# Column vectors laid out by the host, filler turns on TensorE, and a last down projection that finishes quarter by quarter

## The chip, the cores and the metric

One core of one Trainium2 chip runs the program; the other cores are idle. The metric is device time in microseconds of that core, as the median of several runs. The kernel before takes 1831.78 us (median of three runs, 1830.54 to 1832.52). A profile is one further execution of the same program; times inside it count from the start of its span.

## The reference

The function takes x, 256 positions of 2048 fp32 values, through three blocks. The first two (MLA attention, sliding-window attention with sinks) compute `x = x + (y * silu(gate)) @ w_out` on a normalised input. The third runs one more normalised mixer (block attention and a state space part), and then a gated feed-forward block whose output is normalised before it is added to x. What the change touches is the first normalisation,

```
h = rmsnorm(x, layer_norm[0])            # x * rsqrt(mean(x^2) + eps) * g
proj = h @ mla_w_in
```

the small vectors that are used as one scalar per feature (gains of norms, the filters and offsets of two depthwise convolutions), and the very end,

```
down = hidden @ w_ffn_down               # (256, 5632) @ (5632, 2048)
x = x + rms_norm(down, ln_ffn_post)      # gain, and 1/sqrt(mean(down^2) + eps) per row
return x
```

## The kernel before, in words

Every weight matrix streams through TensorE in tiles of 128x1024 fp32. SyncE issues the load of a tile into one of four `raw` slots. ScalarE rounds it to `w_high` (line 1163), VectorE forms `w_low = raw - w_high` (line 1662) and adds one to the semaphore `low_made`. TensorE then multiplies three times (high by high, high by low, low by high) and adds one to `tiles_used`, which frees the slots. `split(tile)` on ScalarE and VectorE always runs three tiles ahead (LEAD = 3). Activations are split into high and low parts in the same way. Each engine has its own program, written out by hand, and the engines meet at semaphores only, so an instruction that waits holds up everything behind it on its engine.

**The start.** SyncE loads the two halves of x (`x_in`), then weight tiles. ScalarE's queue loads the identity matrix (`ident_in`, line 1255) and half of the small vectors, one DMA each, as rows of `vector_rows` (line 1257); GpSimd's queue loads the other half (line 2448). TensorE waits for all of them and turns six groups of rows into columns in PSUM (line 621). VectorE copies those into `column_vectors` (lines 1773 to 1779, with a factor 0.5 on two parts) and adds to `cols_done`; only behind that, on the same engine, stands `normalise0` (line 1675), which scales most of x by its roots. ScalarE scales the rest (line 1188). `transpose_rows` on TensorE turns the scaled x in 32 turns of 128x128 (line 545), four to a PSUM bank. Of each bank ScalarE makes `hT_high` (line 1225) and VectorE `hT_low` (line 1679). The first weight tile is multiplied (lines 515 to 517) behind the 32 turns and once `hl_done` is 2, that is, once two banks have low parts.

**The end.** The down projection sums over 44 chunks of the hidden layer into all eight PSUM banks. Bank 4t + g holds rows t (0 or 1, 128 rows each) and columns 512g to 512g + 511. `down_step` takes 8 tiles: tiles 0 to 3 are the left half of the columns for four chunks, tiles 4 to 7 the right half. In the last step (`last_down_step`) tiles 4 to 7 are multiplied first for t = 0, which completes banks 2 and 3 (`first_rows`), then for t = 1, which completes banks 6 and 7. Behind that stands the output of the block. For each bank ScalarE takes the sum of squares (line 1644, semaphore `sq`) and VectorE the product with the gain into `nx` (line 2437, semaphore `scaled`). The two engines go through the banks in different orders (`ACT_TAIL`, `DVE_TAIL`), and each waits for the other before it takes a bank that the other one had. For rows t, VectorE then adds four sums (line 2418), GpSimd makes the root `rstd` (lines 2568, 2569), VectorE computes `x = nx * rstd + x` in four pieces (line 2423, semaphore `fin`), and SyncE stores each piece (line 491).

Of the kernel before, what the change touches and what calls it, by code (L numbers as in the profile page):

```python
# [24 lines left out]
F32 = mybir.dt.float32  # L25
# [55 lines left out]
LINE = 32  # L81
FIRST_IN = ((T_C, 0), (T_KR, 16), (T_MLAO + LEAD, 0), (T_KV, 16), (T_SWAO + LEAD, 0), (T_XBC, 16),
# [119 lines left out]
def program(nc, a, out, toeplitz):  # L202
# [9 lines left out]
    with ctx:  # L212
# [50 lines left out]
        rows = sb("vector_rows", [P, 6, P], F32, s0)  # L263
# [91 lines left out]
        def column(slot, at):  # L355
# [4 lines left out]
        row_loads = [(0, V_LN0, a["layer_norm"]), (0, V_QN, a["q_norm"]), (0, V_KVN, a["kv_norm"]),  # L360
                     (0, V_MIX, a["ln_mix_pre"]), (0, V_FFN, a["ln_ffn_pre"]), (0, V_SSMN, a["ssm_norm"]),
                     (0, V_XB, a["conv_b"]), (1, 0, a["conv_w"]), (2, 0, a["ffn_b"])]
        row_loads += [(3 + k, 0, a["ffn_w"][88 * k:88 * (k + 1), :]) for k in range(3)]
        N_ROWS = len(row_loads)
# [4 lines left out]
        consts_in, ident_in, vec_in, rows_in = sem("consts_in"), sem("ident_in"), sem("vec_in"), sem("rows_in")  # L369
        rows_in_act, masks_made = sem("rows_in_act"), sem("masks_made")  # L370
# [3 lines left out]
        cols_psum, cols_done, trig_angle, trig_done = sem("cols_psum"), sem("cols_done"), sem("trig_angle"), sem("trig_done")  # L374
# [22 lines left out]
        ff = names("ffn", "ups", "acc", "taps", "gelu", "hidden", "split", "sq", "rs", "scaled", "first_rows", "fin")  # L397
# [3 lines left out]
        DVE_TAIL = (4, 5, 0, 1, 3, 2, 7, 6)  # L401
# [14 lines left out]
        def _(sp):  # L416
# [80 lines left out]
        def _(pe):  # L497
# [614 lines left out]
            def down_rows(i, j, t):  # L1112
# [5 lines left out]
                for k in range(2):  # L1118
# [8 lines left out]
            def last_down_step(i):  # L1127
# [22 lines left out]
        def _(act):  # L1150
# [105 lines left out]
            for slot, row, src in row_loads[:len(row_loads) // 2]:  # L1256
                act.dma_start(rows[row:row + src.shape[0], slot, :], src).then_inc(rows_in_act, 16)
# [4 lines left out]
            normalise1(1)  # L1262
            act.wait_ge(cols_done, 1)
# [383 lines left out]

        @block.vector
        def _(dve):
# [119 lines left out]
            dve.wait_ge(cols_psum, 1)  # L1769
            for slot, n in enumerate((V_SLOT0, 48, FC * 2, FC * 2, FC * 2, FC * 2)):  # L1770
# [831 lines left out]
```

## Time and profile before

| | us |
|---|---|
| median of three runs | 1831.78 |
| the profiled execution, its own time | 1830.33 |
| its span | 1828.5 |
| TensorE busy | 1790.7 |
| VectorE busy | 1139.2 |
| ScalarE busy | 896.3 |
| first weight multiplied | 21.44 |
| last matmul starts | 1819.87 |

"Busy" is the union of an engine's instructions. TensorE appears twice, as PE (the matmuls) and PEld (the loads of its stationary operand, which overlap the matmuls). The duration of a matmul in a row contains its way through the array, so two that follow each other overlap: the distance between starts is what each costs. A row of the timeline gives the start, the duration, the engine, the line, what is written and read, how many instructions are merged, and in brackets how long the engine was idle before and what released it.

### The profile page before, as it was taken

Reading aid. Unit: us, or ns where it says so; the run is one execution under the profiler, and the core shown is the slowest. Engines: PE = TensorE matmul, PEld = TensorE weight load, DVE = VectorE, ACT = ScalarE, POOL = GpSimd, SP = SyncE. Lnnn points to the kernel's source line nnn. Section 1 sums busy time; section 2 is a strip of 40 time slices with the busy share of each in tenths; the row PEclk is TensorE's granted clock in tenths of the full one; section 3 lists DMA queues with packets and bytes.
Section 4 is the critical chain, followed back from the end, with each engine's and each line's share of the span. In section 5 each row is a group of like instructions: output and inputs, shape, how many; then the busy total and the mean of one; then the engine's idle time right before and its main releaser. Section 6 shows DMA issues by size and latency. Waiting matters only on the chain. (4 is left out here: it accounts for less than half of the span.)

```text
span 1828.5 us, 35122 instructions
## 1 busy us (share of the span) xinstructions
PE 1790.7 (98%) x13052; PEld 1671.4 (91%) x13052; DVE 1139.2 (62%) x1790; ACT 896.3 (49%) x1350; POOL 154.3 (8%) x189
## 2 busy tenths in 40 slices
PE   6999999999999999999999999999999999999998
PEld 5999998899999788999999779999999999988886
DVE  6665555656777766766565556666666666644445
ACT  6555454555544555454444445444554444433333
POOL 1001110000100101000000000100000000033321
PEclk9999999999999999999999999999999999999999
DMA  7555555565454455665564655666656666666554
GB/s 234 168 166 152 162 156 173 183 181 179 145 158 155 148 187 168 186 192 168 171 179 144 208 160 178 193 197 192 194 184 189 190 198 193 199 197 193 192 193 139
DMA packets 235612, 326.46 MB, mean 179 GB/s; under 512 B 12432, under 2 KB 170420, under 8 KB 234896
## 3 DMA queue, kind: packets, MB, share of 16 engines
q1 hardware_dynamic: 233440, 318.61, 56.5%
q0 software_dynamic: 1808, 6.69, 1.2%
q8 instruction: 52, 0.85, 0.2%
q14 instruction: 24, 0.20, 0.0%
q10 hardware_dynamic: 288, 0.11, 0.0%
HBM read 323.24 MB, written 2.13 MB: 178 GB/s over the span
## 5 line engine op out<-in xcount | busy, mean ns | idle before, releaser
L1662 DVE TENSOR_TENSOR w_low<-raw,w_high 128x1024 fp32r<-128x1024 f32 x603 | 736.1, 1230 | 573.0 <-ACT w_high L1163 571.4
L1163 ACT CAST w_high<-raw 128x1024 fp32r<-128x1024 f32 x603 | 626.9, 1049 | 645.3 <-PE bank L509 330.4
L507 PE MATMUL bank<-hT_high,w_high 128*128 128x256 f32 x2608 | 728.6, 279 | 6.1 <-DVE hT_low L1679 2.8
L509 PE MATMUL bank<-hT_high,w_low 128*128 128x256 f32 x2608 | 722.7, 277 | 0.0
L508 PE MATMUL bank<-hT_low,w_high 128*128 128x256 f32 x2608 | 722.7, 277 | 0.0
L507 PEld LDWEIGHTS bank<-hT_high,w_high 128*128 128x128 f32 x2608 | 490.8, 188 | 13.2 <-issue 5.8
L509 PEld LDWEIGHTS bank<-hT_high,w_low 128*128 128x128 f32 x2608 | 490.6, 188 | 0.0
L508 PEld LDWEIGHTS bank<-hT_low,w_high 128*128 128x128 f32 x2608 | 490.4, 188 | 0.1
L515 PE MATMUL bank<-w_high,yT_high 128*128 128x512 f32 x384 | 152.2, 396 | 4.8 <-POOL yT_low L2464 2.8
L517 PE MATMUL bank<-w_high,yT_low 128*128 128x512 f32 x384 | 149.8, 390 | 0.0
L516 PE MATMUL bank<-w_low,yT_high 128*128 128x512 f32 x384 | 149.8, 390 | 0.0
L1124 PE MATMUL bank<-w_high,hidden_low 128*128 128x512 f32 x264 | 102.7, 389 | 0.0
L1122 PE MATMUL bank<-w_high,hidden_high 128*128 128x512 f32 x264 | 102.7, 389 | 0.0
L1123 PE MATMUL bank<-w_low,hidden_high 128*128 128x512 f32 x264 | 102.7, 389 | 0.0
L515 PE MATMUL bank<-w_high,hT_high 128*128 128x256 f32 (+1 forms) x320 | 96.8, 303 | 0.0
L516 PE MATMUL bank<-w_low,hT_high 128*128 128x256 f32 (+1 forms) x320 | 96.1, 300 | 0.0
L517 PE MATMUL bank<-w_high,hT_low 128*128 128x256 f32 (+1 forms) x320 | 96.0, 300 | 0.0
L515 PEld LDWEIGHTS bank<-w_high,yT_high 128*128 128x128 f32 x384 | 72.1, 188 | 22.0 <-issue 4.0
L517 PEld LDWEIGHTS bank<-w_high,yT_low 128*128 128x128 f32 x384 | 72.1, 188 | 15.5
L516 PEld LDWEIGHTS bank<-w_low,yT_high 128*128 128x128 f32 x384 | 72.1, 188 | 14.5
L2553 POOL COPY hidden_staged<-hidden_T 128x512 f32 (+1 forms) x22 | 14.5, 658 | 610.7 <-DVE hidden_T L2371 474.7
L2463 POOL CAST yT_high<-y_rows 128x256 f32 (+3 forms) x28 | 17.4, 622 | 552.2 <-DVE y_rows L1833 442.1
(322 smaller groups left out, 2166.7 us busy)
## 6 DMA issues: line engine op xcount, KB each, us to landing
raw<-in_w_up SPq DMA_DIRECT2D x176, 512.0 KB, 4.5
raw<-in_w_in SPq DMA_DIRECT2D x88, 512.0 KB, 3.7
raw<-in_w_down SPq DMA_DIRECT2D x88, 512.0 KB, 4.4
raw<-in_w_swa SPq DMA_DIRECT2D x72, 512.0 KB, 4.1
raw<-in_w_c SPq DMA_DIRECT2D x50, 512.0 KB, 3.8
raw<-in_w_mlao SPq DMA_DIRECT2D x32, 512.0 KB, 3.7
raw<-in_w_swao SPq DMA_DIRECT2D x32, 512.0 KB, 4.4
raw<-in_w_out SPq DMA_DIRECT2D x32, 512.0 KB, 4.0
```

The costliest lines, as they stand in the source:

```text
L507: nc.tensor.matmul(to, h, act_h[:, chunk, :], start=first, stop=False, skip_group_check=True)
L508: nc.tensor.matmul(to, h, act_l[:, chunk, :], start=False, stop=False, skip_group_check=True)
L509: return nc.tensor.matmul(to, l, act_h[:, chunk, :], start=False, stop=last, skip_group_check=True)
L515: nc.tensor.matmul(to, ah, h, start=first, stop=False, skip_group_check=True)
L516: nc.tensor.matmul(to, ah, l, start=False, stop=False, skip_group_check=True)
L517: return nc.tensor.matmul(to, al, h, start=False, stop=last, skip_group_check=True)
L1122: nc.tensor.matmul(to, ah, wh[:, w], start=first, stop=False, skip_group_check=True)
L1123: nc.tensor.matmul(to, ah, wl[:, w], start=False, stop=False, skip_group_check=True)
L1124: last = nc.tensor.matmul(to, al, wh[:, w], start=False, stop=True, skip_group_check=True)
L1163: nc.scalar.copy(whi(tile, i, n), raw[s][:, :]).then_inc(high_made, 1)
L1662: v.tensor_tensor(wlo(tile, i, n), raw[s][:, :], whi(tile, i, n).bitcast(F32), ALU.subtract).then_inc(low_made, 1)
L2463: chain.done(g_.tensor_copy(h, y32[:, 0:n, :]))
```

## The change

Four things change.

The host lays all small vectors out as one array of shape 128 x 6 x 96, as `column_vectors` has it. ScalarE's queue loads the first of the six parts, GpSimd's queue the other five in one DMA; `vector_rows`, its six turns and its copies are gone. VectorE only halves two parts in place.

TensorE runs 44 turns of the identity matrix into bank 7 as soon as `ident_in` has come, ahead of the 32 real turns. Nobody reads them.

In the last down step tiles 4 to 7 are multiplied for one bank at a time: bank 2, bank 3, bank 6, bank 7. `first_rows` now counts the first three.

In the output, VectorE takes the banks in the order in which they are completed, and waits for ScalarE's square of a bank before its own product. The sums and outputs of rows 0 and 1 stand at new places in VectorE's program. The first of the four output pieces of rows 1 is no longer VectorE's: ScalarE multiplies `nx` by the root in place, GpSimd adds x, and SyncE stores that piece third of four.

```diff
+WARM = 44
-        DVE_TAIL = (4, 5, 0, 1, 3, 2, 7, 6)
+        DVE_TAIL = (4, 5, 0, 1, 2, 3, 6, 7)
@@ SyncE
-            for b in range(8):
-                sp.wait_ge(ff["fin"], b + 1)
-                t, g = b // 4, b % 4
+            for n, (t, g) in enumerate(((0, 0), (0, 1), (0, 2), (0, 3), (1, 1), (1, 2), (1, 0), (1, 3))):
+                if (t, g) == (1, 0):
+                    sp.wait_ge(ff["fin_pool"], 1)
+                else:
+                    sp.wait_ge(ff["fin"], n + 1 if n < 6 else 7)
                 sp.dma_start(out[t * P:(t + 1) * P, g * 512:(g + 1) * 512],
@@ TensorE, start
             pe.wait_ge(ident_in, 16)
-            pe.wait_ge(rows_in_act, 16 * (N_ROWS // 2))
-            pe.wait_ge(rows_in, 16 * (N_ROWS - N_ROWS // 2))
-            for slot, n in enumerate((V_SLOT0, 48, 2 * FC, 2 * FC, 2 * FC, 2 * FC)):
-                last = nc.tensor.transpose(banks[slot // 3][:, (slot % 3) * P:(slot % 3) * P + n], rows[0:n, slot, :], ident[0:n, 0:n])
-            last.then_inc(cols_psum, 1)
-            pe.wait_ge(cols_done, 1)
+            for _ in range(WARM):
+                flip(banks[7][:, 0:P], ident)
             transpose_rows()
@@ TensorE, last_down_step (down_rows takes the halves k to do as ks)
-                for j in range(4, 8):
-                    ready(T_DOWN + j, i, 8)
-                    last = down_rows(i, j, 0)
-                last.then_inc(ff["first_rows"], 1)
-                for j in range(4, 8):
-                    down_rows(i, j, 1).then_inc(tiles_used, 1)
+                for t in range(TT):
+                    for k in range(2):
+                        for j in range(4, 8):
+                            if t + k == 0:
+                                ready(T_DOWN + j, i, 8)
+                            last = down_rows(i, j, t, (k,))
+                            if t + k == 2:
+                                last.then_inc(tiles_used, 1)
+                        if t + k < 2:
+                            last.then_inc(ff["first_rows"], 1)
@@ ScalarE, start and output
-            for slot, row, src in row_loads[:len(row_loads) // 2]:
-                act.dma_start(rows[row:row + src.shape[0], slot, :], src).then_inc(rows_in_act, 16)
+            act.dma_start(colv[:, 0, :], a["columns"][:, 0, :]).then_inc(cols_first, 16)
...
-                if n == 4:
-                    act.wait_ge(ff["first_rows"], 1)
-                if n == 6:
+                if n in (4, 5, 6):
+                    act.wait_ge(ff["first_rows"], n - 3)
+                if n == 7:
                     act.wait_ge(tiles_used, T_END)
-                if n in (2, 5, 7):
+                if n == 2:
                     act.wait_ge(ff["scaled"], n)
...
+            act.wait_ge(rstd_done, RSTD_TAIL + 1)
+            act.wait_ge(ff["scaled"], 8)
+            nc.scalar.activation(nx[:, 1, 0:512], nx[:, 1, 0:512], ACT.Copy, scale=rstd[:, 1:2]).then_inc(ff["times_r"], 1)
@@ VectorE, start
-            dve.wait_ge(cols_psum, 1)
-            for slot, n in enumerate((V_SLOT0, 48, FC * 2, FC * 2, FC * 2, FC * 2)):
...
-            last.then_inc(cols_done, 1)
+            dve.wait_ge(cols_first, 16)
+            v.tensor_scalar(colv[:, 0, V_XB:V_SLOT0], colv[:, 0, V_XB:V_SLOT0], 0.5, None, ALU.mult)
+            dve.wait_ge(cols_rest, 16)
+            v.tensor_scalar(colv[:, 1, 0:48], colv[:, 1, 0:48], 0.5, None, ALU.mult).then_inc(cols_done, 1)
             normalise0(1)
@@ VectorE, output (output_rows without its sum, which is row_sums)
+                if n in (2, 4, 5, 6):
+                    dve.wait_ge(ff["sq"], 2 if n == 2 else n + 1)
+                if n == 5:
+                    row_sums(0, 6)
                 if n == 6:
-                    output_rows(0, 6)
-                    dve.wait_ge(tiles_used, T_END)
-                if n in (2, 5, 7):
-                    dve.wait_ge(ff["sq"], n)
-                t, cols = b // 4, slice(b % 4 * 512, (b % 4 + 1) * 512)
-                v.tensor_tensor(nx[:, t, cols], banks[b], gbc[:, cols], ALU.mult).then_inc(ff["scaled"], 1)
-            output_rows(1, 8)
+                    output_rows(0, 6, 0)
+                if n == 7:
+                    row_sums(1, 8)
+                scaled_by_gain(b)
+            output_rows(1, 8, 1)
@@ GpSimd, start and output
-            for slot, row, src in row_loads[len(row_loads) // 2:]:
-                pool.dma_start(rows[row:row + src.shape[0], slot, :], src).then_inc(rows_in, 16)
+            pool.dma_start(colv[:, 1:6, :], a["columns"][:, 1:6, :]).then_inc(cols_rest, 16)
...
+            pool.wait_ge(ff["times_r"], 1)
+            g_.tensor_tensor(x[:, 1, 0:512], nx[:, 1, 0:512], x[:, 1, 0:512], ALU.add).then_inc(ff["fin_pool"], 1)
```

The instruction lists below name an instruction by its line, what it writes and reads, its size, and in brackets the semaphores that it waits for.

TensorE's program at the start, before (the first rows below the start of the block):

```order
L621 MATMUL bank0<-constants,vector_rows 128x92 [waits rows_in,rows_in_act,ident_in]
L621 MATMUL bank0<-constants,vector_rows 128x48
L621 MATMUL bank0<-constants,vector_rows 128x88
L621 MATMUL bank1<-constants,vector_rows 128x88 x3
L545 MATMUL bank0<-constants,nx 128x128 [waits nx_done,cols_done]
```

The same place after the change:

```order
L541 MATMUL bank7<-constants 128x128 [waits ident_in]
L541 MATMUL bank7<-constants 128x128 x43
L541 MATMUL bank0<-constants,nx 128x128 [waits nx_done]
L541 MATMUL bank0<-constants,nx 128x128 x3
L541 MATMUL bank1<-constants,nx 128x128 [waits nx_done]
```

Six turns of vector rows have given way to 44 of the identity, and the first real turn waits for scaled x alone.

VectorE's program at the end, before, from the first product with the gain (`scores` are banks 4 and 5):

```order
L2437 TENSOR_TENSOR nx<-scores,gain_rows 128x512 [waits tiles_used,gain_in]
...
L2437 TENSOR_TENSOR nx<-bank,gain_rows 128x512 [waits ffn_first_rows]
L2437 TENSOR_TENSOR nx<-bank,gain_rows 128x512 [waits ffn_sq]
L2418 TENSOR_REDUCE sum_squares<-small 128x1 [waits ffn_sq]
L2423 SCALAR_TENSOR_TENSOR x<-nx,rstd,x 128x512 [waits rstd_done,ffn_scaled]
L2423 SCALAR_TENSOR_TENSOR x<-nx,rstd,x 128x512 x3
L2437 TENSOR_TENSOR nx<-bank,gain_rows 128x512 [waits tiles_used]
L2437 TENSOR_TENSOR nx<-bank,gain_rows 128x512 [waits ffn_sq]
L2418 TENSOR_REDUCE sum_squares<-small 128x1 [waits ffn_sq]
L2423 SCALAR_TENSOR_TENSOR x<-nx,rstd,x 128x512 [waits rstd_done,ffn_scaled]
L2423 SCALAR_TENSOR_TENSOR x<-nx,rstd,x 128x512 x3
```

The same place after the change, from bank 2 on:

```order
L2423 TENSOR_TENSOR nx<-bank,gain_rows 128x512 [waits ffn_sq]
L2409 TENSOR_REDUCE sum_squares<-small 128x1 [waits ffn_sq]
L2423 TENSOR_TENSOR nx<-bank,gain_rows 128x512
L2417 SCALAR_TENSOR_TENSOR x<-nx,rstd,x 128x512 [waits rstd_done,ffn_scaled,ffn_sq]
L2417 SCALAR_TENSOR_TENSOR x<-nx,rstd,x 128x512 x3
L2423 TENSOR_TENSOR nx<-bank,gain_rows 128x512
L2409 TENSOR_REDUCE sum_squares<-small 128x1 [waits ffn_sq]
L2423 TENSOR_TENSOR nx<-bank,gain_rows 128x512
L2417 SCALAR_TENSOR_TENSOR x<-nx,rstd,x 128x512 [waits rstd_done,ffn_scaled]
L2417 SCALAR_TENSOR_TENSOR x<-nx,rstd,x 128x512 x2
```

The reduction of each half has moved ahead of the product of that half's last bank. The four outputs of rows 0 now wait for a third semaphore, `ffn_sq`: its count is 7, ScalarE's square of bank 6. The product of bank 6 stands behind them.

TensorE's program in the last down step, tiles 4 to 7 (in slots 3, 0, 1, 2), before, without the rows of line 1123:

```order
L1122 MATMUL bank2<-w_high3,hidden_high 128x512 [waits low_made]
...
L1122 MATMUL bank3<-w_high3,hidden_high 128x512
...
L1122 MATMUL bank2<-w_high0,hidden_high 128x512 [waits low_made]
...
L1122 MATMUL bank3<-w_high0,hidden_high 128x512
...
L1122 MATMUL bank2<-w_high1,hidden_high 128x512 [waits low_made]
...
L1122 MATMUL bank3<-w_high1,hidden_high 128x512
...
L1122 MATMUL bank2<-w_high2,hidden_high 128x512 [waits low_made]
```

The same place after the change:

```order
L1114 MATMUL bank2<-w_high3,hidden_high 128x512 [waits low_made]
...
L1114 MATMUL bank2<-w_high0,hidden_high 128x512 [waits low_made]
...
L1114 MATMUL bank2<-w_high1,hidden_high 128x512 [waits low_made]
...
L1114 MATMUL bank2<-w_high2,hidden_high 128x512 [waits low_made]
...
L1114 MATMUL bank3<-w_high3,hidden_high 128x512
```

Between the first matmul of tile 4 and that of tile 7 there stood 18 matmuls; now there stand 9.

## Rows read from the trace of the kernel before

**Rows 1.** The page: busy time, share of the span, instructions, of each engine.

```profile
PE 1790.7 (98%) x13052; PEld 1671.4 (91%) x13052; DVE 1139.2 (62%) x1790; ACT 896.3 (49%) x1350; POOL 154.3 (8%) x189
```

**Rows 2.** Waits in 12 to 26 us: in total, times, longest.

```profile
PE bank L621 <- DMA vector_rows<-in_ssm_norm: 12.1, 1, 12.1
PE bank L545 <- DVE nx L1675: 2.0, 1, 2.0
```

**Rows 3.** Timeline of the start: start, duration, instruction, idle before.

```profile
9.35 1.91 ACT L1260 ACTIVATE nx<-x 128x2048 f32<-128x2048 f32 x1 [0.58 <-DMA x<-in_x]
12.48 1.95 ACT L1188 ACTIVATE nx<-x,rstd 128x512 f32<-128x512 f32 x3 [1.13 <-POOL rstd L2456]
13.57 0.24 DVE L1775 COPY column_vectors<-bank 128x80 f32<-128x80 f32 x1 [13.57 <-PE bank L621]
14.55 2.22 DVE L1675 TENSOR_SCALAR nx<-x,rstd 128x512 f32<-128x512 f32 x5
15.54 3.28 PEld L545 LDWEIGHTS bank<-constants,nx 128*128 128x128 f32 x16 [2.27 <-DVE column_vectors L1779]
16.69 1.70 ACT L1225 ACTIVATE hT_high<-bank,column_vectors 128x256 fp32r<-128x256 f32 x4 [0.98 <-PE bank L545]
17.92 1.65 DVE L1679 SCALAR_TENSOR_TENSOR hT_low<-bank,column_vectors,hT_high 128x256 fp32r<-128x256 f32 x4
18.80 1.72 PEld L545 LDWEIGHTS scores<-constants,nx 128*128 128x128 f32 x8
20.50 0.94 PEld L545 LDWEIGHTS bank<-constants,nx 128*128 128x128 f32 x8
21.42 0.19 PEld L515 LDWEIGHTS bank<-w_high,hT_high 128*128 128x128 f32 x1
```

**Rows 4.** The identity's DMA on ScalarE's queue: its issue, and time to landing.

```profile
L1255 ACTq DMA_DIRECT2D constants<-in_constants x1: 387/387/387, 1.9 to 1.9; - x1
DMA to landing us min/median/max: 8.0/8.0/8.0
```

**Rows 5.** Timeline of TensorE at 1085 us: turns of the identity.

```profile
1085.30 4.09 PE L545 MATMUL scores<-constants 128*128 128x128 f32 x36
```

**Rows 6.** Stretches: busy of PE, PEld, DVE, ACT, POOL, then granted clock, DMA share, GB/s.

```profile
12.00:15.50 3.50, 1.43 (x6) 0.94 (x6) 1.93 (x10) 2.78 (x4) 0.45 (x1) 1.00 1.03 414
18.80:20.62 1.82, 1.82 (x10) 1.82 (x10) 1.82 (x4) 1.82 (x5) 0.00 (x0) 1.00 0.82 203
```

**Rows 7.** Timeline of the last down step and the output.

```profile
1809.22 0.39 PE L1122 MATMUL bank<-w_high,hidden_high 128*128 128x512 f32 x1
1809.47 1.05 ACT L1163 CAST w_high<-raw 128x1024 fp32r<-128x1024 f32 x1 [1.67 <-PE scores L1124]
1810.55 1.23 DVE L1662 TENSOR_TENSOR w_low<-raw,w_high 128x1024 fp32r<-128x1024 f32 x1 [1.49 <-ACT w_high L1163]
1817.50 2.74 DVE L2423 SCALAR_TENSOR_TENSOR x<-nx,rstd,x 128x512 f32<-128x512 f32 x4 [1.04 <-POOL rstd L2569]
1819.87 0.39 PE L1124 MATMUL bank<-w_high,hidden_low 128*128 128x512 f32 x1
1820.30 1.41 DVE L2437 TENSOR_TENSOR nx<-bank,gain_rows 128x512 f32<-128x512 f32 x2
1821.02 0.60 ACT L1644 ACTIVATE hT_high<-bank 128x512 fp32r<-128x512 f32 x1
1821.74 0.16 DVE L2418 TENSOR_REDUCE sum_squares<-small 128x1 f32<-128x4 f32 x1
1822.92 2.74 DVE L2423 SCALAR_TENSOR_TENSOR x<-nx,rstd,x 128x512 f32<-128x512 f32 x4 [1.02 <-POOL rstd L2569]
1825.02 0.99 SPq L491 DMA_DIRECT2D out<-x  x2
```

**Rows 8.** GpSimd's two-input operations on 512 columns: count, busy, mean ns, idle.

```profile
L2555 POOL TENSOR_TENSOR hidden_low<-hidden_staged,hidden_high 128x512 fp32r<-128x512 f32 x22 | 44.7, 2034 | 1.8
L2464 POOL TENSOR_TENSOR yT_low<-y_rows,yT_high 128x512 fp32r<-128x512 f32 x4 | 5.1, 1284 | 0.3
```

More of the change, by code:

```diff
@@ L357, in column @@
             return colv[:, slot, at:at + 1] if isinstance(at, int) else colv[:, slot, bass.ds(at, 1)]
[L360 to L364, printed above, removed]
         raw_loaded = [sem(f"raw_loaded{s}") for s in range(SLOTS)]
         high_made, low_made, tiles_used = sem("high_made"), sem("low_made"), sem("tiles_used")
-        consts_in, ident_in, vec_in, rows_in = sem("consts_in"), sem("ident_in"), sem("vec_in"), sem("rows_in")
-        rows_in_act, masks_made = sem("rows_in_act"), sem("masks_made")
+        consts_in, ident_in, vec_in, cols_first = sem("consts_in"), sem("ident_in"), sem("vec_in"), sem("cols_first")
+        cols_rest, masks_made = sem("cols_rest"), sem("masks_made")
         x_in = [sem("x_in0"), sem("x_in1")]
@@ L396, in program @@
                    "gated", "ss", "rstd", "yn", "y_tr", "y_high", "y_low")
-        ff = names("ffn", "ups", "acc", "taps", "gelu", "hidden", "split", "sq", "rs", "scaled", "first_rows", "fin")
+        ff = names("ffn", "ups", "acc", "taps", "gelu", "hidden", "split", "sq", "rs", "scaled", "first_rows", "fin", "times_r", "fin_pool")
+        RSTD_TAIL = 7
         ACT_TAIL = (0, 1, 4, 5, 2, 3, 6, 7)
-        DVE_TAIL = (4, 5, 0, 1, 3, 2, 7, 6)
+        DVE_TAIL = (4, 5, 0, 1, 2, 3, 6, 7)
         def start(eng, *groups):
@@ L1117, in down_rows @@
                 al = hidl[:, chunk // 2, chunk % 2, t * P:(t + 1) * P]
-                for k in range(2):
+                for k in ks:
                     to = banks[4 * t + 2 * half + k]
@@ L1262, in _ @@
             normalise1(1)
+            act.wait_ge(cols_first, 16)
             act.wait_ge(cols_done, 1)
@@ L1766, in angles @@
                 v.scalar_tensor_tensor(turns[:, :], ang[:, :], -1.0, ang[:, :], ALU.mult, ALU.max).then_inc(trig_angle, 1)
-            dve.wait_ge(cols_psum, 1)
-            for slot, n in enumerate((V_SLOT0, 48, FC * 2, FC * 2, FC * 2, FC * 2)):
-                src = banks[slot // 3][:, (slot % 3) * P:(slot % 3) * P + n]
-                if slot == 1:
-                    last = v.tensor_scalar(colv[:, 1, 0:n], src, 0.5, None, ALU.mult)
-                elif slot == 0:
-                    v.tensor_copy(colv[:, 0, 0:V_XB], src[:, 0:V_XB])
-                    last = v.tensor_scalar(colv[:, 0, V_XB:n], src[:, V_XB:n], 0.5, None, ALU.mult)
-                else:
-                    last = v.tensor_copy(colv[:, slot, 0:n], src)
-            last.then_inc(cols_done, 1)
+            dve.wait_ge(cols_first, 16)
+            v.tensor_scalar(colv[:, 0, V_XB:V_SLOT0], colv[:, 0, V_XB:V_SLOT0], 0.5, None, ALU.mult)
+            dve.wait_ge(cols_rest, 16)
+            v.tensor_scalar(colv[:, 1, 0:48], colv[:, 1, 0:48], 0.5, None, ALU.mult).then_inc(cols_done, 1)
             normalise0(1)
@@ L2414, in _, with row_sums, output_rows @@
             dve.wait_ge(gain_in, 48)
-            def output_rows(t, squared):
+            def row_sums(t, squared):
                 dve.wait_ge(ff["sq"], squared)
                 v.reduce_sum(ss[:, t:t + 1], small[:, 4 * t:4 * t + 4], axis=AX.X).then_inc(ff["rs"], 1)
-                dve.wait_ge(ff["scaled"], squared)
-                dve.wait_ge(rstd_done, 7 + t)
-                for g in range(4):
+            def output_rows(t, scaled, first):
+                dve.wait_ge(ff["scaled"], scaled)
+                dve.wait_ge(rstd_done, RSTD_TAIL + t)
+                for g in range(first, 4):
                     cols = slice(g * 512, (g + 1) * 512)
@@ L2424, in output_rows, with scaled_by_gain @@
                                            ALU.mult, ALU.add).then_inc(ff["fin"], 1)
+            def scaled_by_gain(b):
+                t, cols = b // 4, slice(b % 4 * 512, (b % 4 + 1) * 512)
+                v.tensor_tensor(nx[:, t, cols], banks[b], gbc[:, cols], ALU.mult).then_inc(ff["scaled"], 1)
             for n, b in enumerate(DVE_TAIL):
@@ L2569, in _, with vectors_as_columns @@
                 g_.tensor_tensor(rstd[:, one], rstd[:, one], nhalf[:, one], ALU.pow).then_inc(rstd_done, 1)
+            pool.wait_ge(ff["times_r"], 1)
+            g_.tensor_tensor(x[:, 1, 0:512], nx[:, 1, 0:512], x[:, 1, 0:512], ALU.add).then_inc(ff["fin_pool"], 1)
+def vectors_as_columns(f):
+    slots = [["layer_norm", "mla_q_norm", "mla_kv_norm", "ln_mix_pre_2", "ln_ffn_pre_2", "ssm_norm_w_2", "ssm_conv_b_2"],
+             ["ssm_conv_w_2"], ["ffn_conv_b_2"]]
+    laid = [np.concatenate([f(name).reshape(-1, P) for name in slot]) for slot in slots]
+    laid += list(f("ffn_conv_w_2").reshape(3, 2 * FC, P))
+    out = np.zeros((P, 6, 96), np.float32)
+    for slot, part in enumerate(laid):
+        out[:, slot, :part.shape[0]] = part.T
+    return out
 def kernel(**inputs):
@@ L2581 @@
         "constants": shape_constants(),
[L2582 to L2586 removed]
+        "columns": vectors_as_columns(f),
         "final_norm": f("final_norm").reshape(1, D), "ln_mix_post": f("ln_mix_post_2").reshape(1, D),
```

12 lines of the change are left out of this document (2 added, 10 removed).

## The prediction

> **What bounds the kernel now.** I read the page first. TensorE is busy for 1790.7 of 1828.5 us, 98% of the span, while VectorE is at 62% and ScalarE at 49% [rows 1]. No edit touches the number of matmuls that matter or their pace in between, so only two places can move the time: the 21.4 us ahead of the first weight, and what lies behind the last matmul. I then read the waits and the timeline of the first 26 us. TensorE idles for 12.1 us until the last rows of vectors land and another 2.0 us for scaled x [rows 2]. Scaled x is late because VectorE copies columns from 13.57 and begins to scale at 14.55 only, while the roots were there for ScalarE at 12.48 [rows 3]. From 15.54 on TensorE turns without a pause and the first weight follows at 21.42 [rows 3]: the turns themselves set that moment, not `hl_done` (VectorE's low parts of the first two banks run 17.92 to 19.57).
>
> The pace of the turns matters. Eight loads take from 18.80 to 20.50, 0.2125 us each; the eight behind them take 0.94 us, and 36 turns at 1085 us take 4.09 us, which without the last one's 0.27 us way through the array is 0.11 us each [rows 3, 5]. The granted clock reads 1.00 in the slow stretch too [rows 6], so the column doesn't show it; a factor of two in the pace of equal work is TensorE at 1.2 and then at 2.4 GHz, with the rise at 20.50, after 4.96 us of unbroken turns, or 8.4 us after the first rows were turned at about 12.1. By the Trainium skill ("TensorE: Matmul & The Clock Gate", "What's actually happening") the clock is either of these two and nothing between; rows 3 and 5 agree, the clock column doesn't.
>
> At the end the last matmul starts at 1819.87 and is through at 1820.26. Products and squares of banks 6 and 7 take until 1821.74, sum and root until 1822.92, four outputs until 1825.66, and the last store is issued at 1825.69 (two issues in 0.99 us from 1825.02, 0.33 each) [rows 7]. The span ends 2.81 us later, at 1828.5. From the last matmul to the end it is 8.24 us.
>
> **The start, part by part.** The vector DMAs: nothing but the columns themselves hangs on them now. VectorE's two halvings can wait for them only if they land after 12.48; the identity, first on the same queue as before, was issued at 1.88 and landed 8.0 us later, at 9.9 [rows 4], and the last rows of before, issued much later, had landed at 12.1. I cost this at nothing. If the one larger GpSimd transfer did land late, the fillers below would hide up to some 3.5 us of it. The copies on VectorE go, so scaling starts at 12.5 in place of 14.55: two microseconds that would all come back if TensorE stood ready.
>
> It doesn't. The 44 fillers start with the identity at 9.9. With a slow stretch of 4.96 us, 23.3 of them run at 0.2125 us; the other 20.7 take 2.28 us at 0.11. They end at 17.1. Scaled x has been complete since about 14.9 (12.5 + 2.22 + what ScalarE adds). The 32 real turns take 3.52 us at 0.11, so the first weight comes at 20.64, 0.78 us earlier than 21.42. Behind it: the first bank is turned at about 17.8, and by the distances of rows 3 (ScalarE 16.69, VectorE's fourth low part at 19.57, at most 2.9 us) `hl_done` is 2 by 20.4 to 20.7, just in time. **I take 0.8 us gained.**
>
> Bounds. If the clock counts from the first work of all, 8.4 us slow: 39.5 fillers slow, 4.5 fast, end at 18.8, first weight at 22.3, a loss of 0.9. All 76 turns slow: 16.15 us, first weight at 26.0, a loss of 4.6. All fast: 8.36 us, first weight at 18.3, a gain of 3.2. I take the unbroken 4.96 us, since the six turns of before were followed by 2 us of idling and the fillers are not. A second unknown is when the identity lands: GpSimd's queue now puts 246 KB of columns and then the positions beside x early, where it spread them before. At 400 GB/s [rows 6] 280 KB more ahead of it are 0.7 us, straight from the gain.
>
> **The end, part by part.** *The last tile is asked for too early.* Tiles 4 to 7 were 18 matmuls apart from first to last, now 9. At 0.227 us (48 matmuls of 0.227 from 1809.22 give the end) TensorE wants tile 7 at 1809.22 + 9 x 0.227 = 1811.26. ScalarE can round it only from 1809.47, when its slot is free, and VectorE has its low part at 1810.55 + 1.23 = 1811.78 [rows 7]. Before, it was wanted at 1813.3 and this was hidden. So TensorE stops for 0.5 us and more: I take 0.55, and all four quarters end that much later, the last at 1820.81. Ends: 0.3 (if the release comes ahead of the modelled end of the operation) and 0.75 (if the 0.19 us of a weight load come on top).
>
> *VectorE's queue.* With quarters 2.72 us apart, bank 6 is complete at 1818.09 and squared 0.75 us later, at 1818.84 (before, 0.72 from 1820.30 to 1821.02). The outputs of rows 0 now wait for that square. Before they ran at 1817.50. They take 2.74, until 1821.58, and the product of bank 6 stands behind them (0.7, until 1822.28), and the sum of rows 1 behind that. ScalarE has squared bank 7 by 1821.56, so the sum waits for VectorE, not for ScalarE. From a sum to the first output it is 1.18 us (1821.74 to 1822.92): outputs of rows 1 begin at 1823.46, against 1822.92. The product of bank 7 hides in those 1.18 us. The freed swap of banks (0.7) is given back here. Three outputs instead of four end at 1825.53, against 1825.66.
>
> *The piece on ScalarE and GpSimd.* ScalarE needs the same root: 1823.46, plus 0.7 (a third of 1.95 and its tail [rows 3]), plus 0.1 for the hand-over, is 1824.26. GpSimd then adds 512 columns of two inputs. It took 2.03 us beside a VectorE that read two inputs for half of the time, and 1.28 us in four others [rows 8]. Here VectorE's outputs read two inputs until 1825.53, so I take 2.15, a bit above the mean, and keep 1.28 as the low end; GpSimd is done at 1826.41 (1825.54). The Trainium skill ("GPSIMD Engine Reference", "Engine selection") says outright that elementwise work of two inputs belongs on VectorE, GpSimd being about twice as slow, and ("Specifications") that VectorE's two-input instructions contend with it. By that alone, twice VectorE's 0.67 us would be some 1.35 us, and contention more; row 8 has both.
>
> *The stores.* SyncE stores that piece third of four and waits for it, so the last store, ready at 1825.53, is issued behind it: 1826.44 + 0.33 = 1826.77, against 1825.69, that is 1.08 later. Two stores of 256 KB now leave 0.33 us apart where it was 0.67, so the last queues by another 0.35 or so. **The end costs 1.4 us** (1.08 + 0.35), 0.55 of it the stop of TensorE. Ends: 0.2 (GpSimd at 1.28, a stop of 0.3, little queueing) and 1.8.
>
> **The sum.** -0.8 + 1.4 = +0.6 us. On the profiled execution's 1830.33 that is 1830.9; the median of before lies 1.45 above that execution, so on its scale I expect 1831.78 + 0.6 = 1832.4. Anything within 3.66 us (0.2%) is no change, about what a measurement of this kernel can tell.
>
> **The rivals.** *A: the warm start pays in full.* The clock rises early in the fillers, or the identity lands well before 9.9. Then the first weight comes up to 3.2 us earlier. With the cost at the end: 1831.78 - 3.2 + 1.4 = 1830.0; with the cheapest end, 1828.8; only with the identity also 1 us early is it past 0.2%. For it: the pace doubled within one turn in before, so a rise can be anywhere. Against it: 4.96 us of unbroken work were not enough until 20.50.
>
> *B: the end pays.* GpSimd is at 1.28 us and TensorE hardly stops: +0.2 - 0.8, 1831.2. For it: four rows at 1.28. Against: 22 rows at 2.03, and VectorE active beside it.
>
> *C: the fillers run slow to the last one, and the real turns as well.* One mechanism, in front of the first weight: TensorE stays at 1.2 GHz through turns of 128 columns. Price 4.6 us, plus 1.4: 1837.8, slower. It is past 0.2% once the first weight comes later than about 23.7, that is, once the slow stretch lasts 11 us. For it: before ran slow until 8.4 us after its first work. Against it: the unbroken part of that was 4.96 us.
>
> *D: the slow stretch lasts 8.4 us,* by the same evidence: +0.9 + 1.4, 1834.1.
>
> **How the numbers follow.** The forecast, with its own range of 1831.0 to 1833.5: 64%. A: 12%, B: 10%, D: 7%, C: 4%; 3% for what I don't see. The two ends outside 0.2% are C, and A where all its luck comes together. The range has to take in A at 1830.0, D at 1834.1, and the 2 us by which the three runs of before differ among themselves: 1829.6 to 1834.8. Faster by over 0.2%: 6%; within: 88%; slower: 6%.
>
> **What would show it.** The first weight between 20 and 21.2 us, ahead of it turns at 0.11, and fillers that start at 9.9 and double their pace midway. A gap of about 0.5 us in TensorE ahead of the matmuls of tile 7. Outputs of rows 0 that begin behind the square of bank 6 and end after the last matmul; VectorE's last sum more than 1 us behind the last matmul; GpSimd's addition ending after VectorE's last output; the last store issued 6 us after the last matmul (before 5.4). I am wrong if the fillers are over by 14 us, if TensorE doesn't stop at tile 7, or if rows 0 are out before bank 6 is squared.

## The result, and the profile after

The kernel before takes 1830.69 us (median of 20 runs, 1829.6 to 1834.11), the changed one 1833.43 us (20 runs, 1832.15 to 1836.54). The ratio is 1.0014, 95% interval 1.0008 to 1.002: 2.7 us or 0.14% slower, inside the 0.2% that the prediction called no change, and on the side of its +0.6 us. In the runs of the last experiments two timings, 5644.21 us (e10) and 2581.43 us (the kernel before beside it), lie far out; they count in the medians and not in the ratios. The profiled executions differ by 2.85 us: 1833.18 against 1830.33 in their own time, spans 1831.1 against 1828.5.

I cut both traces at two moments, the first weight and the end of the last matmul (start plus 0.39 us):

| us | before | after | difference | forecast |
|---|---|---|---|---|
| start of the span to the first weight | 21.42 | 23.01 | +1.59 | -0.78 |
| first weight to the end of the last matmul | 1798.84 | 1799.71 | +0.87, of it 0.71 the stop at tile 7 | +0.55 |
| end of the last matmul to the end of the span | 8.24 | 8.38 | +0.14 | +0.85 |
| outside the span | 1.83 | 2.08 | +0.25 | 0 |
| sum | 1830.33 | 1833.18 | +2.85 | +0.62 |

The start. Timeline of the changed kernel, one engine after the other (start, duration, instruction, idle before), to be read beside [rows 3]:

```profile
5.63 1.91 ACT L1255 ACTIVATE nx<-x 128x2048 f32<-128x2048 f32 x1 [1.36 <-DMA x<-in_x]
10.50 1.91 ACT L1255 ACTIVATE nx<-x 128x2048 f32<-128x2048 f32 x1 [2.87 <-DMA x<-in_x]
13.63 1.95 ACT L1184 ACTIVATE nx<-x,rstd 128x512 f32<-128x512 f32 x3 [1.13 <-POOL rstd L2454]
12.99 0.17 DVE L1769 TENSOR_SCALAR column_vectors<-column_vectors 128x12 f32<-128x12 f32 x1 [12.99 <-DMA column_vectors<-in_columns]
13.63 2.07 DVE L1674 TENSOR_SCALAR nx<-x,rstd 128x512 f32<-128x512 f32 x5 [0.37 <-POOL rstd L2454]
11.99 7.55 PEld L541 LDWEIGHTS bank<-constants 128*128 128x128 f32 x44 [11.99 <-DMA constants<-in_constants]
19.52 1.78 PEld L541 LDWEIGHTS bank<-constants,nx 128*128 128x128 f32 x16
23.01 0.19 PEld L511 LDWEIGHTS bank<-w_high,hT_high 128*128 128x128 f32 x1
```

The copies are gone, yet scaling begins at 13.63 and not at 12.5: the second half of x is squared from 10.50 on, where it was 9.35 [rows 3]. The identity lands at 11.99, so the fillers, which need 7.55 us, end at 19.52; scaled x has been complete since 15.7. Between them the fillers hold the real turns up by 3.8 us. The pace is 0.2125 us a turn and then 0.11 [rows 3, 5]: 44 turns in 7.55 us put 26.5 of them at the first pace, 5.6 us.

What landed when, from the DMA issues of the first 14 us (KB each, median us from issue to landing), first the kernel before and then the changed one:

```profile
x<-in_x SPq DMA_DIRECT2D x2, 1024.0 KB, 6.6
positions_i<-in_positions POOLq DMA_DIRECT2D x1, 128.0 KB, 6.6
```

```profile
x<-in_x SPq DMA_DIRECT2D x2, 1024.0 KB, 7.1
column_vectors<-in_columns POOLq DMA_DIRECT2D x1, 240.0 KB, 7.2
positions_i<-in_positions POOLq DMA_DIRECT2D x1, 128.0 KB, 8.3
constants<-in_constants ACTq DMA_DIRECT2D x1, 64.0 KB, 10.1
```

The identity, 8.0 us underway before [rows 4], now needs 10.1. In 5 to 9.2 us GpSimd's queue (q0) takes 45% of the DMA engines where it took 18%, and less is moved in all (335 against 362 GB/s). DMA queues in that stretch (packets, MB, share of 16 engines), before and after:

```profile
q1 hardware_dynamic: 248, 1.23, 75.5%
q0 software_dynamic: 179, 0.21, 18.3%
```

```profile
q1 hardware_dynamic: 151, 1.00, 57.7%
q0 software_dynamic: 92, 0.36, 45.0%
```

The end. Timeline of the changed kernel from the last tile on, to be read beside [rows 7]:

```profile
1811.22 1.05 ACT L1159 CAST w_high<-raw 128x1024 fp32r<-128x1024 f32 x1 [1.67 <-PE scores L1116]
1812.30 1.23 DVE L1661 TENSOR_TENSOR w_low<-raw,w_high 128x1024 fp32r<-128x1024 f32 x1 [1.50 <-ACT w_high L1159]
1812.78 0.39 PE L1116 MATMUL bank<-w_high,hidden_low 128*128 128x512 f32 x1
1813.58 0.50 PE L1114 MATMUL bank<-w_high,hidden_high 128*128 128x512 f32 x1 [0.41 <-DVE w_low L1661]
1820.03 0.60 ACT L1640 ACTIVATE hT_high<-bank 128x512 fp32r<-128x512 f32 x1 [2.03 <-PE bank L1116]
1820.76 2.74 DVE L2417 SCALAR_TENSOR_TENSOR x<-nx,rstd,x 128x512 f32<-128x512 f32 x4 [1.90 <-ACT hT_high L1640]
1822.33 0.39 PE L1116 MATMUL bank<-w_high,hidden_low 128*128 128x512 f32 x1
1823.41 0.68 DVE L2423 TENSOR_TENSOR nx<-bank,gain_rows 128x512 f32<-128x512 f32 x1
1824.01 0.14 DVE L2409 TENSOR_REDUCE sum_squares<-small 128x1 f32<-128x4 f32 x1
1825.11 0.72 ACT L1644 ACTIVATE nx<-nx,rstd 128x512 f32<-128x512 f32 x1 [1.67 <-POOL rstd L2567]
1825.18 3.08 DVE L2417 SCALAR_TENSOR_TENSOR x<-nx,rstd,x 128x512 f32<-128x512 f32 x3 [0.42 <-POOL rstd L2567]
1825.91 1.80 POOL L2569 TENSOR_TENSOR x<-nx,x 128x512 f32<-128x512 f32 x1 [0.83 <-ACT nx L1644]
```

Tile 7 is wanted at 1812.78 + 0.23 = 1813.01; its low part is made until 1813.53, and the matmul starts at 1813.58. (The wait shows as 0.41 us because the row counts from the modelled end of the matmul before.) From the first matmul of tile 4 at 1810.97 to the end of the last it is 11.75 us; in before it is 1819.87 + 0.39 - 1809.22 = 11.04 for the same 48 matmuls [rows 7], so the stop costs 0.71 us. Outputs of rows 0 run from 1820.76, behind the square of bank 6, and hold up the product of bank 6 and, behind it, the sum. The sum runs at 1824.01, 1.29 us behind the end of the last matmul at 1822.72. The piece on ScalarE and GpSimd is done at 1827.71, VectorE's third output only at 1828.26.

### The profile page after: what moved, and what is told of

Same layout as the page of the kernel before. It is cut to its first block and busy times, and to the rows that moved or that the text cites. A ratio compares the mean times of both kernels' runs of the same rounds, so it can differ in the third digit from the quotient of the medians.

```text
span 1831.1 us, 35184 instructions
## 1 busy us (share of the span) xinstructions
PE 1794.7 (98%) x13090; PEld 1675.5 (92%) x13090; DVE 1139.0 (62%) x1784; ACT 896.4 (49%) x1351; POOL 153.9 (8%) x185
```

## The experiments

Each kernel is the changed one with the edit shown (e4 apart); "..." marks what is left out. Where a kernel was timed, its ratio is to the kernel before. "Middle" is the stretch from the first weight to the end of the last matmul, "output" the one from there to the end of the span.

**The start.** *e1: no fillers.*

```diff
-WARM = 44
+WARM = 0
```

> The changed kernel without its 44 filler turns. Theory 1 (the fillers hold back the real turns, for which scaled x is there from about 14.4 us): the real turns start at 14.4, run slow (0.2125 us) for the 5.5 us that the fillers took to speed up, 26 of the 32, then 0.11: first weight at 20.6 us in place of 23.0, span 2.4 us shorter, about 1828.7. Theory 2 (the fillers pay for themselves, what is late is the identity alone): the first weight comes no earlier than 23.0, or comes earlier and its matmuls run at half pace, so that the span is unchanged at 1831. Between them, all 32 turns slow: 21.4.

Measured: 1831.15 us (10 runs) against 1830.82 of before (25 runs), ratio 1.0003 (0.9993 to 1.0013). Weight loads of its trace:

```profile
14.46 3.27 PEld L541 LDWEIGHTS bank<-constants,nx 128*128 128x128 f32 x16 [14.46 <-issue]
17.71 1.53 PEld L541 LDWEIGHTS scores<-constants,nx 128*128 128x128 f32 x8
19.21 0.90 PEld L541 LDWEIGHTS bank<-constants,nx 128*128 128x128 f32 x8
20.09 0.19 PEld L511 LDWEIGHTS bank<-w_high,hT_high 128*128 128x128 f32 x1
```

The real turns begin as soon as scaled x is there, pay the slow stretch themselves (about 22 slow turns, 4.5 us), and still the first weight comes at 20.09. The fillers don't save the slow stretch; they move it ahead, behind a load that lands late, and add their own 44 turns. Against the 23.01 of the changed kernel's trace that is 2.9 us; against e7 (below), which has the same fillers and its first weight at 21.04, it is 1.0. The timings alone don't tell e1 from the changed kernel: each was set against the kernel before in another series, with ratios of 1.0003 (up to 1.0013) and 1.0014 (from 1.0008).

*e2: GpSimd issues the positions and the sinks only when x is in.*

```diff
+            pool.wait_ge(x_in[1], 16)
             pool.dma_start(posi[:, :], a["positions"]
```

> The changed kernel, but GpSimd issues its loads of the positions (128 KB) and of the sinks only once x has landed. Theory 1 (GpSimd's early transfers take turns with x and with the identity): 144 KB less ahead of them, x complete 0.4 us earlier than 10.5 and the identity 0.4 to 1.0 us earlier than 12.0, first weight 0.4 to 1.0 earlier. Theory 2 (the identity is late because of the transfer behind it on ScalarE's queue, or by chance): x at 10.5 and the identity at 12.0 as before.

Start of its timeline:

```profile
9.19 1.91 ACT L1255 ACTIVATE nx<-x 128x2048 f32<-128x2048 f32 x1 [1.30 <-DMA x<-in_x]
9.41 7.18 PEld L541 LDWEIGHTS bank<-constants 128*128 128x128 f32 x44 [9.41 <-DMA constants<-in_constants]
20.05 0.19 PEld L511 LDWEIGHTS bank<-w_high,hT_high 128*128 128x128 f32 x1
```

The identity lands 2.6 us earlier than in the changed kernel's trace and x 1.3 us earlier, by taking 144 KB out of the way. Other traces agree: the identity needs 9.1 to 10.1 us to land in the five with the positions early (the changed kernel, e1, e5, e6, e7) and 7.4 to 7.6 in the four with them late (e2, e8, e9, e10). Their bytes would be about 0.36 us at 400 GB/s [rows 6]. The direction was right, and the size several times what bytes say. The span was 1831.3 all the same: this trace's middle has two spells of half pace that before's hasn't (last section).

*e3: GpSimd issues all its loads when x is in.*

```diff
+            pool.wait_ge(x_in[1], 16)
             pool.dma_start(colv[:, 1:6, :], a["columns"]
```

> The changed kernel, but GpSimd issues all its loads (246 KB of columns, positions, sinks) only once x has landed. Theory 1: nothing of GpSimd's runs beside x, so x is complete by 9.3 us or a bit earlier and the identity lands at 9.9 or earlier (before: 9.9); fillers from there, first weight at 9.9 + 5.5 + 2.0 + 3.5 = 20.9, span 2.1 us shorter than 1831.1, about 1829.0. Risk: the columns land only at 12 to 13 us and hold VectorE's scaling back; the fillers hide up to 3 us of that. Theory 2 (ScalarE's queue or chance): identity at 12.0, no change.

Measured: 1832.28 us (10 runs), ratio 1.0006 (0.9996 to 1.0015). The identity lands at 8.78, and now the columns are late:

```profile
15.40 0.19 DVE L1771 TENSOR_SCALAR column_vectors<-column_vectors 128x48 f32<-128x48 f32 x1 [5.53 <-DMA column_vectors<-in_columns]
16.44 1.73 PEld L541 LDWEIGHTS bank<-constants,nx 128*128 128x128 f32 x16 [0.36 <-DVE nx L1674]
```

VectorE can scale only behind its halving of the columns, so the first weight comes at 20.33. It is the positions that have to move, not the columns.

**The end.** *e4: the kernel before with the new end only* (order of tiles 4 to 7, VectorE's order, the piece and the stores; the start untouched).

```diff
-        DVE_TAIL = (4, 5, 0, 1, 3, 2, 7, 6)
+        DVE_TAIL = (4, 5, 0, 1, 2, 3, 6, 7)
...
+                            last = down_rows(i, j, t, (k,))
...
-            output_rows(1, 8)
+            output_rows(1, 8, 1)
```

> The kernel before with only the new end (quarters, new order on VectorE, one piece on ScalarE and GpSimd). Theory 1 (of the 2.6 us that the span grew, 1.6 are the start, 0.7 a stop of TensorE ahead of tile 7, 0.14 the output): first weight at 21.4, span 1828.5 + 0.85 = 1829.4, last matmul through to end of span 8.4 us. Theory 2 (the end is as good as before and the growth is all the start or the stretch between): span 1828.5.

Measured: 1832.57 us (10 runs), ratio 1.0005 (0.9995 to 1.0015). The trace has the first weight at 21.66 and the same stop at tile 7:

```profile
1812.55 0.39 PE L1127 MATMUL bank<-w_high,hidden_low 128*128 128x512 f32 x1
1813.35 0.50 PE L1125 MATMUL bank<-w_high,hidden_high 128*128 128x512 f32 x1 [0.41 <-DVE w_low L1672]
```

Its output takes 8.62 us. The span is 1831.1; without one such spell in its middle (1.6 us, last section) it would be about 1829.5, near the 1829.4 expected. So the new end alone isn't told apart from before, and neither is the changed kernel without its fillers (e1). The new start with the old end was not run.

*e5: the outputs of rows 0 ahead of the wait for the square of bank 6.*

```diff
+                if n == 6:
+                    output_rows(0, 6, 0)
                 if n in (2, 4, 5, 6):
                     dve.wait_ge(ff["sq"], 2 if n == 2 else n + 1)
                 if n == 5:
                     row_sums(0, 6)
-                if n == 6:
-                    output_rows(0, 6, 0)
```

> The changed kernel, with the four outputs of rows 0 ahead of the wait for ScalarE's square of bank 6 in VectorE's program. Theory 1 (these outputs, started 1.96 us before the last matmul is through, hold back the sum of rows 1): they start 1.2 us after the sum of rows 0, are over before the last matmul, and the sum of rows 1 comes 0.78 us behind the end of the last matmul (now 1.29), so that the span ends 7.9 us behind it (now 8.38). Theory 2 (the output is bound by something later, GpSimd or the stores): the distance from the last matmul to the end stays 8.4. Only distances from the last matmul on count here.

In its trace the last matmul is through at 1825.18, and the sum of rows 1 runs at

```profile
1825.94 0.16 DVE L2409 TENSOR_REDUCE sum_squares<-small 128x1 f32<-128x4 f32 x1 [0.83 <-ACT hT_high L1640]
```

0.76 us behind it, against 1.29 in the changed kernel, and it waits for ScalarE now. Output 7.82 us (8.38 before the edit): the queue on VectorE was real and cost about half a microsecond.

*e6: rows 0 by tile, as before, and only rows 1 by quarters.*

```diff
-                for t in range(TT):
-                    for k in range(2):
-                        for j in range(4, 8):
...
+                for j in range(4, 8):
+                    ready(T_DOWN + j, i, 8)
+                    last = down_rows(i, j, 0)
+                last.then_inc(ff["first_rows"], 2)
+                for k in range(2):
+                    for j in range(4, 8):
+                        last = down_rows(i, j, 1, (k,))
...
```

> The changed kernel, but tiles 4 to 7 of the last down step are multiplied for rows 0 as before (both banks for a tile, then the next tile), and quarter by quarter for rows 1 only. Theory 1 (asking for tile 7 after 9 matmuls in place of 18 costs 0.7 us): no wait on w_low in the last step, and 11.04 us from the first matmul of tile 4 until the last one is through, as before, in place of 11.75; the output behind it unchanged at 8.4 us. Theory 2: the gap only moves, 11.5 or more.

In its trace TensorE waits for no low part any more; first matmul of tile 4 and last matmul:

```profile
1811.36 0.39 PE L1114 MATMUL bank<-w_high,hidden_high 128*128 128x512 f32 x1
1822.01 0.39 PE L1116 MATMUL bank<-w_high,hidden_low 128*128 128x512 f32 x1
```

That is 11.04 us to the end, as expected: the 0.71 us stop comes from the quarters of rows 0 alone. The output behind it is unchanged at 8.40.

*e7: no piece on ScalarE and GpSimd; VectorE does all four outputs, stored in order.*

```diff
-            output_rows(1, 8, 1)
+            output_rows(1, 8, 0)
...
-            nc.scalar.activation(nx[:, 1, 0:512], nx[:, 1, 0:512], ACT.Copy, scale=rstd[:, 1:2]).then_inc(ff["times_r"], 1)
-            g_.tensor_tensor(x[:, 1, 0:512], nx[:, 1, 0:512], x[:, 1, 0:512], ALU.add).then_inc(ff["fin_pool"], 1)
```

> The changed kernel, but VectorE makes all four outputs of rows 1, with nothing on ScalarE and GpSimd and the stores in order. Theory 1 (GpSimd's addition makes VectorE's last output take 1.75 us in place of 0.75, so the fourth piece elsewhere gains nothing): four outputs of 0.67 us, over 2.74 us after their start in place of 3.08, and 8.0 us from the last matmul to the end in place of 8.38. Theory 2 (a piece taken off VectorE is a piece gained): 0.67 us more on VectorE than its present 3.08, so 9.0 us.

Its trace:

```profile
1825.31 2.74 DVE L2411 SCALAR_TENSOR_TENSOR x<-nx,rstd,x 128x512 f32<-128x512 f32 x4 [0.42 <-POOL rstd L2561]
```

VectorE makes four outputs in 2.74 us where three beside GpSimd took 3.08 (in the changed kernel and in e1 to e6 alike). Output 7.95 us against 8.38: the piece, with its place in the stores, costs 0.4 us.

**All of it together.** *e8 has the edits of e1, e2, e5, e6 and e7; e9 is the same kernel, timed; e10 has 16 fillers (`WARM = 16`) in place of none.*

> Columns from the host kept; no fillers; positions and sinks loaded only once x is in; rows 0 of the last step by tile; rows 0 out before the wait for bank 6; four outputs on VectorE. Theory 1: x at 9.2, real turns from 13.3, first weight 5.6 us later at 18.9; 1798.8 us to the end of the last matmul as in the kernel before, if the clock stays up between; 7.55 us of output (sum at 0.78, first output 1.18 later, 2.74 for four, 2.85 to the end). Span 1825.3, plus 1.2 to 1.7 for each stretch in the middle in which TensorE's clock falls. Theory 2 (parts overlap, what one gives another takes): 1827.5 or more even with the clock up.

> The kernel of e8 again, timed, since a single run can't tell 3 us from the stretches of low clock in the middle. Theory 1 (start 2.7 us and output 0.8 us shorter than in the kernel before, nothing given back): median 3.0 to 3.5 us below the kernel before and 5.5 to 6.5 below the changed kernel. Theory 2 (an earlier first weight is lost again in the middle, as e2 and e3 could be read, where the first weight came 1.4 and 1.1 us earlier than in before and the span was longer): median no more than 1 us below the kernel before.

> The kernel of e9 with 16 fillers ahead of the real turns. Theory 1 (fillers are good as far as they end before scaled x is there, at 13.3 us): they start with the identity at 9.4, run slow until 12.8, the clock rises 3.9 to 5.5 us after their start, at 13.3 to 14.9, so that most real turns are fast; then the low parts of the first two banks set the first weight, about 18.0, 0.7 us earlier than without fillers. Theory 2 (the pause of half a microsecond between fillers and real turns undoes them): turns slow for another 4 us, first weight at 18.7 or later.

e8: first weight 18.70, output 7.42, span 1825.7 (1825.3 expected). e9: 1828.35 us (11 runs) against 1831.55 of before (21 runs), ratio 0.9983 (0.9974 to 0.9992). e10: 1827.48 us (11 runs), ratio 0.998 (0.997 to 0.9989). So both beat the kernel before, by 3.2 and 4.1 us, and are not told apart from each other. By the segments of its trace e9 gains 3.3 us ahead of the first weight and 0.8 in the output, and loses 0.2 outside the span. How much of the start is owed to the columns from the host, and how much to moving the positions, wasn't separated. e10's weight loads:

```profile
9.33 3.27 PEld L538 LDWEIGHTS bank<-constants 128*128 128x128 f32 x16 [9.33 <-DMA constants<-in_constants]
13.17 2.14 PEld L538 LDWEIGHTS bank<-constants,nx 128*128 128x128 f32 x16 [0.57 <-DVE nx L1669]
18.08 0.19 PEld L508 LDWEIGHTS bank<-w_high,hT_high 128*128 128x128 f32 x1 [1.02 <-DVE hT_low L1673]
```

Sixteen fillers are over when scaled x comes, the 0.57 us of idling behind them don't undo them, the real turns run slow for four turns only, and then the first weight waits 1.02 us for VectorE's low parts. Against 18.14 (e9) and 18.70 (e8) that is a gain of 0.1 to 0.6 us: a right-sized warm start can't give more here, since `hl_done` comes next. In the timings that gain isn't told from nothing.

## Why the prediction was right, and where its steps were off

**The time.** +0.6 us forecast, +2.7 measured, both inside 0.2%; the forecast's own range (1831.0 to 1833.5) holds 1833.43 at its very end. That is luck. The range stood on a median of 1831.78 for the kernel before, from three runs; 20 runs give 1830.69. On that base the same forecast is 1831.3 and the same range 1829.9 to 1832.4, and 1833.43 lies outside it. The sign of the whole came out right by luck too, with a start that went the wrong way: forecast -0.8, measured +1.6, while the end cost 0.85 us in place of 1.4. The 0.2% that counted as no change are 3.66 us wide, more than all of these.

**The start (the term of -0.8).** "The fillers start with the identity at 9.9" failed: it landed at 11.99. The mechanism was named as the second unknown (GpSimd's 246 KB and the positions beside x), but sized by bytes, at 0.7 us; it is 2.1 us in this trace, and e2 takes 2.6 us back. Within the start, 2.1 us are the late identity, 0.3 us the longer slow stretch (5.6 against 4.96 us, in which half of the turns are done all the same); 20.64 + 2.1 + 0.3 is the 23.01 measured, to 0.03 us. 23.01 is the late end of what this start does: e5, e6 and e7, with the same start, have the identity at 11.05 to 11.53, fillers of 6.19 to 7.45 us, and the first weight at 21.96, 21.61 and 21.04. So the start is worth between -0.4 and +1.6 us, and e7's 21.04 is as early as the forecast had it (20 to 21.2), by a slow stretch of 2.8 us behind an identity at 11.38. That the real turns run at 0.11 behind the fillers and that `hl_done` isn't late was right. Rival D asked for a slow stretch of 8.4 us and C for one without end; A for an identity before 9.9 or an early rise. None of them happened in the changed kernel's trace; the early rise did in e6 and e7 (last section), against a late identity.

**The stop at tile 7 (0.55).** Right in place and cause (e6), 0.71 in size: 0.57 until the matmul starts, and some 0.1 more in the restart (the next one begins 0.34 us later, where 0.227 is the pace), which I had put in the upper bound only.

**VectorE's queue.** Sum of rows 1 forecast 1.47 us behind the last matmul, measured 1.29; e5 (0.76) shows that rows 0 held it up.

**The piece.** GpSimd's addition was put at 2.15 us and took 1.80, so it no longer ends behind VectorE. What the prediction missed is the other side: VectorE's last output took 1.75 us, where the other six of that line took 0.75. That output, and the last two stores, in the changed kernel:

```profile
1826.51 1.75 DVE L2417 SCALAR_TENSOR_TENSOR x<-nx,rstd,x 128x512 f32<-128x512 f32 x1
1827.74 0.88 SPq L487 DMA_DIRECT2D out<-x  x2
```

The Trainium skill ("SBUF — State Buffer", "Who interferes with whom") says that VectorE and GpSimd share a pair of ports under an exclusive lock, and that a VectorE instruction with two SBUF inputs contends there with a GpSimd instruction that reads SBUF. The rows fit that, if each waits for the other's instruction to end: GpSimd's addition would run from VectorE's end at 1826.5 and, at the 1.28 us of [rows 8], be done at 1827.8 (measured 1827.71); VectorE's last output would run from 1827.71 and be done 0.75 us later, at 1828.46 (measured 1828.26). That the slow output comes with the piece is shown (e7); that the ports are the reason rests on that page and these two sums.

**The stores.** The extra 1.08 + 0.35 us for the third store and the queueing didn't come: GpSimd was done before VectorE, the third store was issued at 1827.74 and the last at about 1828.3, 5.6 us behind the last matmul (5.4 in before); the issues end at 1828.62, with 2.5 us to the end, as in before. Net of the stop, the end costs 0.14 us in the profiled execution where 0.85 was forecast.

**Outside the span.** 2.08 us (median of the runs) against 1.82 before, not foreseen. It goes with the new start (e1 2.07, e3 2.11, e9 2.03, e10 2.08; e4 with the old start 1.82). Single runs of the changed kernel spread from 1.78 to 2.18, those of before from 1.77 to 1.88. Which part of the new start does it wasn't separated.

## What to carry over

Before filling a wait with warming work, ask what the filler waits for and when it ends. Fillers that began late and ran on past the arrival of the data cost 1.0 to 2.9 us here; those that were over in time gained 0.1 to 0.6 us in traces, and nothing that the timings tell. Size a load that is issued beside a critical one by moving it away, not by its bytes. Giving one piece of a series to GpSimd while VectorE reads two inputs slows both, and can end later than leaving it. And where a forecast is an absolute time, its base needs as many runs as the difference is small: three runs put this one 1.1 us too high, nearly twice the change that was forecast.

## What the runs showed of the hardware

**The clock drops in the middle, and that is much of the scatter.** In nine of the twelve traces TensorE falls to half pace for seven or eight matmuls of 512 columns, or more of smaller ones, behind a pause of 1.8 to 2.4 us, near 605, 800 or 1013 us; each such stretch is called a spell here. It begins with the first matmul behind the pause or up to six matmuls later. Matmuls of e1, to be set against those of before at the same place:

```profile
1012.58 0.79 PE L511 MATMUL bank<-w_high,yT_high 128*128 128x512 f32 x1 [2.38 <-POOL yT_low L2462]
1013.17 0.63 PE L512 MATMUL bank<-w_low,yT_high 128*128 128x512 f32 x1
1013.60 0.63 PE L513 MATMUL bank<-w_high,yT_low 128*128 128x512 f32 x1
...
1015.71 0.39 PE L512 MATMUL bank<-w_low,yT_high 128*128 128x512 f32 x1
```

```profile
1014.40 0.50 PE L515 MATMUL bank<-w_high,yT_high 128*128 128x512 f32 x1 [2.37 <-POOL yT_low L2464]
1014.74 0.40 PE L516 MATMUL bank<-w_low,yT_high 128*128 128x512 f32 x1
1014.98 0.40 PE L517 MATMUL bank<-w_high,yT_low 128*128 128x512 f32 x1
```

The pause is the same (2.38 and 2.37 us), and one runs on at 2.4 GHz, the other at 1.2 GHz with starts 0.43 us apart. Here the granted clock shows it, unlike in the slow stretch of the start, where it reads 1.00 [rows 6]; stretches of e2 (busy of PE, PEld, DVE, ACT, POOL, then granted clock, DMA share, GB/s):

```profile
600.00:604.00 4.00, 2.01 (x18) 1.27 (x17) 3.15 (x15) 1.04 (x1) 2.41 (x4) 1.00 0.76 246
604.00:608.00 4.00, 4.00 (x13) 3.17 (x12) 2.58 (x9) 2.90 (x10) 0.00 (x0) 0.61 0.40 140
```

and of the changed kernel near 1100 us:

```profile
1096.00:1100.00 4.00, 4.00 (x23) 4.00 (x22) 3.32 (x8) 0.68 (x3) 0.00 (x0) 0.57 0.02 4
```

Middles, less the 0.71 us stop where a kernel has it, by the number of such spells: none, 1798.8 to 1799.6 us (before, the changed one, e8); one, 1800.1 to 1801.2 (e1, e3, e4, e6, e7, e10); two, 1802.2 to 1802.5 (e2, e5, e9). That is some 1.6 us a spell. (One more near 1100 us is in every trace and cancels; the changed kernel's clock is 0.57 in 1096 to 1100 us.) Seven of e9's 11 runs have a mean granted clock of 0.998 and a median span of 1825.9 us, the four at 0.996 and 0.997 one of 1828.05. The split isn't as clean everywhere: of the 25 runs of before beside e1, 7 at 0.998 have a median span of 1828.7, 17 at 0.997 one of 1829.1 and one at 0.996 has 1831.4. A single trace's total therefore says little about an edit of a microsecond; its segments do. What decides whether a pause brings a spell stays open, and so does whether an edit at the start makes them likelier: before's profiled execution has none, e2's two.

**The slow stretch of the start varies.** From the first unbroken turn to the rise it was 4.96 us in before, 5.6 in the changed kernel, about 4.5 in e1, 4.8 in e2, 3.9 in e8 and 3.2 in e9, the last two the same kernel. Four traces with the same start, 44 fillers and the positions early, have 5.6 (the changed kernel), 5.4 (e5), 3.7 (e6) and 2.8 (e7), by the durations of their fillers. The Trainium skill ("TensorE: Matmul & The Clock Gate", "What's actually happening") says that the number of slow matmuls differs from run to run of one kernel; these agree. A sum that rests on it to 0.1 us, as mine did, claims more than can be had.

**A small load can cost several times its bytes.** 144 KB on GpSimd's queue moved the identity's landing by 2.6 us and x's by 1.3 (e2), and the other traces with and without it side by side agree (e2 above). Whether it is the form of the positions' load or the queue that does it wasn't tested.
